# Layer 1 gate units: both parts of the input in one matmul, and the sum of two bank halves

## The reference, cut to what matters

```python
h = rms_norm(x, mix_norm[l])
(u_a, q_b, f_b, i_b, og_b, cx_c, v_c, o_c, ig_c, fg_c, gates) = jnp.split(h @ w_in[l], splits, axis=-1)
...                                   # y_a: S5, y_b: HGRN2, y_c: mLSTM mixers
g_a, g_b, g_c = (gates[..., :D_MODEL], gates[..., D_MODEL:2 * D_MODEL], gates[..., 2 * D_MODEL:])
merged = (jax.nn.sigmoid(g_a) * (y_a @ wb[:r_a])
          + jax.nn.sigmoid(g_b) * (y_b @ wb[r_a:r_b])
          + jax.nn.sigmoid(g_c) * (y_c @ wb[r_b:]))
x = x + merged @ w_out[l]
```

## Time and profile before

| | |
|---|---|
| runs | 2978.95, 2976.33, 2976.12 us; median 2976.33 |
| span of the profiled execution | 2978.0 us, 1.7 us above the median |
| TensorE busy | 99% of the span |
| VectorE busy | 2051.0 us, 69%; in the gate stage far more |
| ScalarE busy | 1311.7 us, 44% |
| HBM | 178 GB/s over the span |

### The profile page before, as it was taken

How to read it: one execution, slowest core, us unless ns; L and a number is a source line. 1 busy time by engine, 2 the same in 40 slices (tenths; PEclk the granted TensorE clock), 3 DMA queues, 4 the chain that set the end, 5 groups by cost and what they waited for, 6 DMA issues and landing times.

```text
span 2978.0 us, 47097 instructions
## 1 busy us (share of the span) xinstructions
PE 2946.2 (99%) x18616; PEld 2630.0 (88%) x18616; DVE 2051.0 (69%) x2624; ACT 1311.7 (44%) x1418; POOL 70.0 (2%) x72
## 2 busy tenths in 40 slices
PE   8999999999999999999999999999999999999999
PEld 8898898999988888888888888876998888888888
DVE  6675787977788888885557776636666666666444
ACT  5354423444444444444444354425445444444333
POOL 0000000000001000000000000000000000000000
PEclk9999999999999999999999999999999999999999
DMA  6553334555555555555555544531555555555555
GB/s 230 184 183 134 114 120 149 168 173 198 186 196 193 189 196 194 190 182 190 193 195 198 195 172 168 186 122 43 184 198 186 195 197 188 193 197 177 194 193 184
DMA packets 87359, 530.39 MB, mean 178 GB/s; under 512 B 9952, under 2 KB 10336, under 8 KB 41184
## 3 DMA queue, kind: packets, MB, share of 16 engines
q1 hardware_dynamic: 87264, 529.07, 50.7%
HBM read 526.94 MB, written 2.10 MB: 178 GB/s over the span
## 4 chain that ended last, share of the span: by engine, by line
PE 96%; DVE 2%; ACT 1%; DMA 0%; issue 0%; SPq 0%; DVEq 0%; ACTq 0%
PE bank L576 74%; PE late L576 22%; DVE arena L1687 1%; DVE w_low L1687 0%; DVE half_low L1687 0%; DVE arena L1684 0%; ACT w_high L1203 0%; PE late L1144 0%; DVE arena L1989 0%; DMA ring<-in_w_gates 0%; DMA xT<-in_xT 0%; DVE acts_both L1687 0%; DVE arena L2045 0%; DVE arena L2016 0%; DVE xrs L1734 0%
## 5 line engine op out<-in xcount | busy, mean ns | idle before, releaser
L1687 DVE TENSOR_TENSOR w_low<-ring,w_high 128x2048 fp32r<-128x2048 f32 (+1 forms) x480 | 1014.3, 2113 | 384.1 <-ACT w_high L1203 380.2
L1203 ACT ACTIVATE w_high<-ring 128x2048 fp32r<-128x2048 f32 (+1 forms) x480 | 849.5, 1771 | 636.0 <-DMA ring<-in_w_down 223.0
L576 PE MATMUL bank<-up_early,w_high 128*128 128x512 f32 x1408 | 487.8, 389 | 0.0
L576 PE MATMUL bank<-up_late,w_high 128*128 128x512 f32 x1408 | 487.3, 389 | 0.0
L576 PE MATMUL late<-acts_both,w_high 128*128 128x512 f32 x1408 | 479.0, 389 | 0.3 <-DVE w_low L1687 0.3
L576 PE MATMUL bank<-up_early,w_low 128*128 128x256 f32 x1408 | 388.6, 276 | 0.0
L576 PE MATMUL late<-acts_both,w_low 128*128 128x256 f32 x1408 | 388.6, 276 | 0.0
L576 PE MATMUL bank<-up_late,w_low 128*128 128x256 f32 x1408 | 388.6, 276 | 0.0
L576 PEld LDWEIGHTS bank<-up_early,w_high 128*128 128x128 f32 x1408 | 264.5, 188 | 55.2
L576 PEld LDWEIGHTS late<-acts_both,w_high 128*128 128x128 f32 x1408 | 264.3, 188 | 55.1 <-DVE w_low L1687 0.6
L576 PEld LDWEIGHTS bank<-up_late,w_high 128*128 128x128 f32 x1408 | 264.0, 188 | 54.7
(11 more groups left out here) (311 smaller groups left out, 4946.2 us busy)
## 6 DMA issues: line engine op xcount, KB each, us to landing
ring<-in_w_up SPq DMA_DIRECT2D x176, 1024.0 KB, 4.7
ring<-in_w_down SPq DMA_DIRECT2D x128, 704.0 KB, 4.0
ring<-in_w_in SPq DMA_DIRECT2D x66, 1024.0 KB, 4.7
ring<-in_w_mix SPq DMA_DIRECT2D x62, 1024.0 KB, 4.8
ring<-in_w_gates SPq DMA_DIRECT2D x96, 512.0 KB, 3.7
ring<-in_w_branch SPq DMA_DIRECT2D x16, 1024.0 KB, 4.7
ring<-in_w_out SPq DMA_DIRECT2D x16, 1024.0 KB, 4.8
ring<-in_w_o SPq DMA_DIRECT2D x16, 1024.0 KB, 4.8
```

The costliest lines, as they stand in the source:

```text
L576: return nc.tensor.matmul(o, lhsT, rhs, start=first, stop=last)
L1203: A(w_high[:, s, 0:cols], ring[:, s, 0:cols], ACT.Copy).then_inc(rounded[s], 1)
L1687: return V.tensor_tensor(o, a, b, op)
```

## The change

A gate unit uses both halves of its bank. The rounded weights meet low and high input in one matmul of 512 columns: `h_both` is one view over both places, `h_low` its first and `h_high` its second part, a fixed distance apart. Half 0 of the bank holds high weights x low input plus low weights x high input, half 1 holds high x high. Per gate 16 matmuls of 512 columns and 16 of 256 take the place of 48 of 256.

ScalarE's `gate(c)` copies bank half 0 into the gate's tile; VectorE's new `sum_gate(c)` adds half 1 and releases the bank (`drained`). It stands ahead of the lowering of gate c+2. ScalarE takes the sigmoid in place two units on, `gate_function(c-2)` behind the copy of gate c, and the last two after gate 47. VectorE's additions for gates 46 and 47 stand ahead of `y_low`. `half_high` is moved up by 64 bytes, with a pad behind the ring.

```diff
@@ tensors
         ring_base = nc.sbuf_base - RING * UNIT * 4
+        sb("ring_pad", [P, P // 4])
...
-        h_high, h_low = alias("h_high", arena_base, [P, KT, T], 46), alias("h_low", hT_base, [P, KT, T])
+        h_apart = (arena_base - hT_base) // (4 * T) + 46
+        assert h_apart * 4 * T == arena_base - hT_base + 46 * 4 * T
+        h_both = alias("h_both", hT_base, [P, 2, h_apart, T])
+        h_low, h_high = h_both[:, 0, 0:KT], h_both[:, 1, 0:KT]
...
-        half_high = alias("half_high", ring_base, [P, RING, HALF], 2 * UNIT // T)
+        half_high = alias("half_high", ring_base, [P, RING, HALF], 2 * UNIT // T, H_SHIFT)
@@ TensorE, gate()
-                        mm(bank[at][:, 0], half_high[:, s, c], h_high[:, k], k == 0, False)
-                        mm(bank[at][:, 0], half_high[:, s, c], h_low[:, k], False, False)
+                        mm(bank[at][:], half_high[:, s, c], h_both[:, :, k], k == 0, False)
@@ ScalarE
+            summed = []
+
             def gate(c):
 
                 halves.next(False, True)
-                s, _, _, there, _ = halves.next(True, True)
+                s, _, _, there, free = halves.next(True, True)
                 act.wait_ge(half_consumed[s], there)
+                summed.append((s, free + 1))
                 at = gate_tile(c)
-                A(arena[:, at * T:(at + 1) * T], bank[s][:, 0], ACT.Sigmoid).then_inc(drained[s], 1)
+                A(arena[:, at * T:(at + 1) * T], bank[s][:, 0], ACT.Copy).then_inc(gate_copied, 1)
+                if c >= 2:
+                    gate_function(c - 2)
+
+            def gate_function(c):
+
+                at = gate_tile(c)
+                act.wait_ge(drained[summed[c][0]], summed[c][1])
+                A(arena[:, at * T:(at + 1) * T], arena[:, at * T:(at + 1) * T], ACT.Sigmoid)
...
             gate(GATES - 1)
+            for c in (GATES - 2, GATES - 1):
+                gate_function(c)
@@ VectorE
+            def sum_gate(c):
+
+                s, at = (2 * c + 1) % RING, gate_tile(c)
+                tile = arena[:, at * T:(at + 1) * T]
+                dve.wait_ge(gate_copied, c + 1)
+                tt(tile, tile, bank[s][:, 1], ADD).then_inc(drained[s], 1)
+
+            lowered_gates = [0]
+
             def lower_gate():
+                c = lowered_gates[0]
+                lowered_gates[0] += 1
+                if c >= 2:
+                    sum_gate(c - 2)
                 for half in range(2):
...
+            sum_gate(GATES - 2)
+            sum_gate(GATES - 1)
             for m, at in enumerate((Q0, O0)):
                 dve.wait_ge(y_rounded, m + 1)
```

More of the change, by code:

```diff
@@ L59 @@
 W_SHIFT = 960
+H_SHIFT = 64
 LATE = 12
@@ L373, in build @@
         half_consumed = [sem(f"half_consumed{s}") for s in range(RING)]
+        gate_copied = sem("gate_half_copied")
         silu_pair, ff_done, conv_made = sem("silu_pair"), sem("ff_act_done"), sem("ff_conv_made")
```

## The result

| | before | after |
|---|---|---|
| median of the runs | 2976.22 us (2973.45 to 2978.95) | 3031.84 us (3030.01 to 3034.14) |
| ratio | 1 | 1.0187, 95% interval 1.0172 to 1.0201 |
| span of the profiled execution | 2978.0 us | 3029.7 us |

The change makes the kernel 1.9% slower; the forecast was 2972.8 us in a range of 2966 to 2981. First the page of after: its span, the busy engines (against the earlier trace rows), the granted clock over the forty slices, and two of its costliest groups (busy us, mean ns | idle before).

What follows compares the result with a forecast made beforehand. TensorE and VectorE were taken to bound the gate stage by stretches, VectorE becoming the bound in the S5 blocks. Terms -1.3 + 1.7 - 2.9 - 2.6 + 1.6 = -3.5 us gave 2972.8 us, range 2966 to 2981.

Steps and rivals of the forecast that it cites:

- The pair, 0.34: Gate units: a 512-column matmul and a 256-column one take 0.34 us together, as in up units; 5.44 us per unit.
- the 0.32: Time each gate unit saves on TensorE, 5.76 to 5.44 us; 15.4 us over 48 if TensorE were the bound everywhere.
- Steps 1 to 3: Four gates from 300.90 us, -1.3; VectorE's chain from 340.35 and gate 8, +1.7; gates 9 to 17, -2.9 us.
- stretch 1: From 300.90 to 340.35 us: four gates where TensorE sets the time, 4 x 0.32 = -1.3 us.
- the +1.7: 340.35 to 382.23 us and gate 8: four additions in VectorE's chain, then gate 8 starting behind addition 6, +1.7 us together.
- Step 4, the S5 blocks: Gates 18 to 47: VectorE becomes the bound, three blocks go from 133.6 to 131.7; -2.6 us over the step.
- rival C: S5 blocks: late VectorE stalls TensorE, delaying ring slots and roundings, so waits stay; +9.5 instead of -2.6, 2985 us; chance 0.12.
- Step 5: End of gates: `y_low` behind addition 47, TensorE waits 3 us; of 2.7 won only 1.1 is left, +1.6 us.
- rival D: Clock falls again behind new waits at last S5 output and branch: +1.7 to +3.4, 2974.5 to 2976.5 us; chance 0.15.
- Rival A: Gate stage: TensorE stays the bound, additions vanish in unseen slots, up to 15.4 us won, 2961 to 2966; chance 0.12.
- B: Gate units: matmuls gain nothing, a pair costs 0.36 as three of 256 columns do; 2978.5 us; chance 0.06.

Runs made afterwards that it cites:

- the kernel without pad: The changed kernel without the pad and without the 64-byte shift of the rounded half slots: 2984.81 us, ratio 1.0012 to before.
- the placed one: The changed kernel with a pad of 256 bytes instead of 128 and `H_SHIFT` 192 instead of 64: 2977.43 us, ratio 1.0005 to before.
- The kernel with the tail in order: On top of the placed one, gate 47 copied before branch weights are rounded, `y_low` ahead of the last two additions: 2975.76 us, ratio 0.9986.
- the last two kernels: The placed one (2977.43 us) and The kernel with the tail in order (2975.76 us).

## Why the prediction was wrong, point by point

**The step that failed** is the sentence "The 64-byte shift I cost at zero". It priced one half of an edit, gave it no bounds and no rival, and left out the other half, the pad, altogether. The pad alone cost 48 us (3028.33 against a median of 2980.43 for before beside it), by a slower pace of matmuls in stages with which the prediction didn't deal. Two things in before could have given a bound. The first is the same instruction at another pace in the same kernel, the first input projection, where 512 columns follow 512 (weights are streamed there):

```profile
110.00 0.40 PE L576 MATMUL bank<-w_low,mix_high 128*128 128x512 f32 x1
110.24 0.40 PE L576 MATMUL bank<-w_high,mix_low 128*128 128x512 f32 x1
110.47 0.40 PE L576 MATMUL bank<-w_high,mix_high 128*128 128x512 f32 x1
```

0.235 us from start to start, against the 0.22 of the earlier trace rows (0.227 by the mean of the stage): width alone doesn't set the pace. Placement has a part in this row too: with the pad alone the same matmuls start 0.229 apart. The second is the constant `W_SHIFT = 960` itself, which says that somebody chose a place. A layer has 1408 pairs of its up stage and 704 of its down stage, both layers 4224; the 15 ns between the two printed steps on each would be 63 us, the 8 ns between the means 34 us: an end of the range on the slow side that was missing. The measured loss in these four stages is 18.6 + 4.6 + 28.0 = 51.2 us.

By the Trainium skill, TensorE: Matmul & The Clock Gate, section Back-to-back issue gap, matmuls that nothing else holds up would start 216 and 109 ns apart by its formula at full clock, an estimate of 325 ns for a pair. No placement here reached it: 340.3 at best, 353.6 at worst.

**The pair, 0.34.** The second size that was off. The chain of the kernel without pad, in the scan, where TensorE alone sets the time:

```profile
381.31 7.41 PE bank L581 x32
388.72 2.68 PE late L581 x24
391.40 5.59 PE bank L581 x32
```

A gate (391.40) takes 5.59 us, not 5.44; 5.60 in after, 5.57 in the placed one. Before it was 5.75. So 0.16 to 0.18 us is won per unit, half of the 0.32. The timeline says which part:

```profile
498.16 1.11 PE L581 MATMUL bank<-h_both,half_low 128*128 128x256 f32 x8
499.11 1.32 PE L581 MATMUL bank<-h_both,half_high 128*128 128x512 f32 x5
```

Five of 512 columns: (1.32 - 0.40) / 4 = 0.23 apart; eight of 256: (1.11 - 0.28) / 7 = 0.12. The reason given, "because width and weights are the same", overlooked that in an up unit the two widths alternate, while in a gate unit eight of 512 follow each other; and "no row exists" went too far, since the rows above at 110 us have 512 columns in a row, at 0.235. By them the unit would have been 16 x 0.355 = 5.68, and the truth lies between the two. Placement of the gate weights moved it only from 5.57 to 5.60, so most of the 0.13 that is left over the 5.44 is not a matter of these distances. Whether it is owed to the order of the widths or to the two halves of the input lying far apart, no run shows.

**Steps 1 to 3.** Measured from the first gate matmul, so that the earlier stages are out, in the kernel without pad:

| from the first gate matmul to | before | gates without pad | difference | forecast |
|---|---|---|---|---|
| end of gate 8 | 86.9 | 88.3 | +1.4 | +0.4 |
| end of gate 15 | 145.9 | 146.2 | +0.3 | -1.8 |
| first S5 output | 208.1 | 208.4 | +0.3 | -2.0 |
| third branch unit | 386.9 | 388.3 | +1.4 | -3.5 |

VectorE's chain starts 0.6 us earlier instead of 1.3 (four units of 0.16). Gate 8 waits for the addition as forecast and then takes 7.41 us for 5.59, a price of 1.8 for the fall of the clock as in the earlier trace rows. Windows over it (length, busy time of each engine, granted clock, DMA share, GB/s):

```profile
381.30:383.30 2.00, 1.99 (x5) 1.62 (x6) 2.00 (x2) 0.00 (x0) 0.00 (x0) 0.58 0.00 0
...
383.30:386.00 2.70, 2.70 (x13) 2.29 (x12) 2.70 (x4) 0.00 (x0) 0.00 (x0) 0.68 0.03 6
...
386.00:389.00 3.00, 3.00 (x20) 2.70 (x19) 2.93 (x5) 0.24 (x1) 0.00 (x0) 1.00 0.53 165
```

Here the prediction's sum has two slips of its own. The start of gate 8 "at about 382.3" has the 1.3 us of stretch 1 in it already, and so has the +1.7 at its end; the sum subtracts the 1.3 once more. By its own terms the first row of the forecast is +1.7, not +0.4, and the whole -2.2 instead of -3.5, that is 2974.1 us. The other slip works the other way. In before, gate 8 waited for half of VectorE's lowering as well; now it waits for the addition ahead of it alone. From the chains of before and of the kernel without pad:

```profile
381.07 1.11 DVE half_low L1687
```

```profile
380.95 0.31 DVE arena L1704
```

So VectorE's stretch is 42.0 us against 41.9 (339.29 to 381.31, 340.35 to 382.23): four additions came in, 1.11 us went out, and the forecast counted the additions alone. With both put right the forecast for the end of gate 8 is about +0.6. The four gates ahead, which won half of the 0.32 each, add 0.6 to it, and gate 8 itself 0.15: that is the +1.4.

The scan's levels then take 8.28 us instead of 8.44, the 0.16 of the unit. VectorE's lead was not used up, as foreseen.

**Step 4, the S5 blocks: right in kind.** The addition's cost is the forecast 0.34, seen in the kernel without pad (compare):

```profile
544.57 0.42 DVE L1704 TENSOR_TENSOR arena<-arena,bank 128x256 f32<-128x256 f32 x1
544.91 1.22 DVE L1704 TENSOR_TENSOR half_low<-ring,half_high 128x1024 fp32r<-128x1024 f32 x1
```

VectorE becomes a bound beside TensorE. In before TensorE has 99% of the chain between 508.9 and 641.4 us; in the kernel without pad TensorE has 54% of it, VectorE 40%, and the transfers and roundings of gate weights 4%. Windows of two blocks (busy: TensorE, weight loads, VectorE, ScalarE), then VectorE's waits for roundings in the first of them (us, times, longest):

```profile
547.66:592.67 45.01, 44.50 (x275) 37.40 (x274) 43.30 (x48) 20.09 (x30) 0.00 (x0) 1.00 0.54 165
592.67:637.00 44.33, 43.81 (x260) 36.89 (x260) 43.81 (x49) 20.06 (x30) 0.00 (x0) 1.00 0.53 168
```

```profile
DVE half_low L1704 <- ACT half_high L1403: 1.6, 3, 0.8
```

VectorE was busy 41.07 of 45.02 and waited 3.5 us for roundings; now it is busy 43.30 and waits 1.6. The three blocks take 132.6 us from first to last S5 output (508.81 to 641.43), 133.7 before (509.06 to 642.75), 131.7 forecast: the waits shrank but didn't vanish, and 1.1 us was won of the 1.9. The loop of rival C went no further than that; it didn't close.

**Step 5 and rival D, the tail: both came.** The chain of the kernel without pad at the end of the gates:

```profile
663.16 1.91 ACT w_high L1207
...
665.79 3.34 DVE y_low L1704 x2
669.13 2.22 DVE w_low L1704
671.39 3.92 PE bank L581 x18
675.31 2.12 PE late L581 x18
677.43 2.12 PE bank L581 x18
```

Rounding, copy, addition, `y_low`, lowering, in the order that the prediction wrote down, with 2.79 us of TensorE waiting before 671.39 (3 forecast). Its times don't fit its sum, though: the sum had won 5.1 us by then (-1.3 + 1.7 - 2.9 - 2.6), while step 5 goes on from glu matmuls that end at 667.7, 2.7 us before the 670.4 of before. By the times of step 5 the second branch unit comes 1.1 us earlier, not 3.5. So the whole would be 2972.8 us by the one and 2975.2 by the other; the range has room for both. Behind it the first 18 matmuls cost 3.92 us, the next 2.12: the clock was at 0.58 and 0.56 in the windows behind the wait, as behind gate 8:

```profile
671.40:673.40 2.00, 2.00 (x10) 0.58 0.99 418
673.40:675.40 2.00, 2.00 (x13) 0.56 0.94 397
675.40:677.40 2.00, 2.00 (x20) 1.00 0.04 8
```

That is 1.8 us, the price of D, in the second of the two places which it named. With the wait it turns the -0.8 us at which the last S5 output stood (341.0 us from the first gate matmul, 341.8 before) into +1.4 at the third branch unit. The kernel with the tail in order has this chain:

```profile
667.53 1.57 ACT arena L1491 x4
669.11 1.81 ACT w_high L1208
670.94 2.30 DVE w_low L1705
673.29 2.40 PE bank L582 x18
...
684.86 3.54 PE bank L582 x30
```

It is before's own chain again, `y_low` is off it, TensorE waits 1.55 us as in the earlier trace rows, the clock doesn't fall, and the third unit starts at 684.86, 2.9 us earlier than in the placed kernel (687.76) and than in before (687.80). The first branch unit has no wait ahead of it. So step 5's cost is shown, by taking it away: 3.0 us from the first gate matmul on, where 3 to 4 were expected.

**The sum with the measured terms.** Gate stage to the third branch unit: +1.4 without pad, -0.6 placed, -3.6 placed and with the tail in order, +2.4 in after. The last but one looks like the forecast of -3.5, and is so by luck. In before the clock also fell once in stretch 1, and one gate took 7.45 us there for 5.76; the kernel without pad and after have such a fall too (7.35 for a gate at 308.74 and at 311.60), the last two kernels have none. Windows of TensorE over that place, in before and in the kernel with the tail in order:

```profile
317.80:321.20 3.40, 3.40 (x19) 0.51 0.10 40
```

```profile
317.80:321.20 3.40, 3.40 (x20) 1.00 0.18 69
```

That is 1.7 us of their gain, which no term of the change explains; without it they stand at about +1.1 and -1.9. In after it is the other way round: the clock fell once more, at 370.46, where 24 matmuls took 4.57 us for the 2.69 of the kernel without pad, and its gate 8 ends 1.0 us later for it.

```profile
370.46:375.04 4.58, 4.57 (x24) 0.63 0.21 77
```

Rival A fell: the gate units won half of what it needs, and VectorE has 40% of the blocks' chain. B fell too, though half of it is true. The kernel as changed left the range by the pad alone.

## What to carry to other kernels

An edit of memory placement, a pad of a few bytes included, is priced like any other edit: find every tensor that moves against another which TensorE reads in the same stretch, and look in the trace for the same matmul at another pace before writing zero. When the busy time of an untouched group grows with its count unchanged, compare its step from start to start in both kernels, and run the pad alone first. A step for a matmul is taken from a row with the same order of widths and the same arrangement of its inputs, and where there is none it gets bounds. A running sum is checked against the start of one marker, such as the last matmul of a stage, so that no gain is counted twice. And what is added for VectorE or ScalarE at a stage's end should stand behind the work that the next stage waits for.

## What the runs showed of the hardware

- TensorE's pace depends on where its two operands lie to each other, modulo 256 bytes: pairs of 512 and 256 columns took 340.3, 347.1, 350.3 or 353.6 ns at full clock in the up stage of layer 1, and both kinds of weights must be well placed for the shortest. In this kernel it is 50 us of 2976. It is so while no other engine and no transfer runs (353.3 ns against 340.0).
- These two distances don't fix the pace alone: one kernel had 353.6 ns in layer 1 and 349.2 in layer 2, and the down stage of layer 1 has two paces at one placement, 340.8 and 350.6 ns for a pair, 7 us. What chooses between them is open.
- The place that is best for one stage isn't for all: with the pad the stages ahead of the gates took 4.0 to 5.4 us less (296.9 with the pad alone, 295.5 in after, 300.9 before), and 512-column matmuls of the input projection started 0.229 us apart instead of 0.235.
- At the distances 0 and 64, a matmul of 512 columns in the up stage, where the widths alternate, took 0.227 us to the next start, and one in the gate units, where eight follow each other, 0.233 to 0.235. With the pad the up stage has 0.233 as well, so one such figure doesn't hold for another stage or placement.
- After waits of TensorE of 3.06 us (gate 8) and 2.79 us (branch) the granted clock went to the lower of its levels, each time at a cost of 1.8 us; after one of 1.55 us it stayed at 1.00. The length of the last wait doesn't decide it: after one of 1.82 us it fell in after (370.46) and after one of 1.84 us at the same point of the kernel without pad (375.31) it stayed. In before it fell at 317.8 as well, with TensorE busy without a pause over 0.1 us since a wait of 1.67 us that ended at 295.13.
